# A new order for the preparation of the next head in the attention stage of a hybrid diffusion step

## The chip, the cores and the metric

One core of one Trainium2 chip runs the whole program. The metric is the device time of one execution in microseconds (us). TensorE is called PE below, VectorE DVE, ScalarE ACT, GpSimd POOL and SyncE SP; PEld is the weight load of PE.

## The reference

One transformer-like layer over 1024 latent and 128 context tokens, width 1024, in float32. It is: a modulated RMSNorm, one input projection, two branches (latent attention with 8 heads, and a gated linear recurrence), a gated merge, an output projection, and a convolutional gated MLP. Only the attention matters here:

```python
q  = (rmsnorm(pq, g_q) @ w_uq).reshape(B, T, 8, 64 + 32)       # rotary on the last 32, latent tokens only
kv = (ckv_keys @ w_ukv).reshape(B, K, 8, 64 + 64)               # keys (64) and values (64); K = 1152 for latents
s  = einsum('bqhd,bkhd->bhqk', q_nope, k_nope) + einsum('bqhr,bkr->bhqk', q_rope, k_rope)
p  = softmax(s * scale);  o = einsum('bhqk,bkhd->bqhd', p, v)
```

## The kernel before

The program runs its stages one after the other, with a barrier of all engines between them: setup, input projection with the recurrence, attention (`stage_attention`), merge, output projection with the MLP. The change touches the attention stage alone.

Float32 products are made as three products in a reduced format (high x high, high x low, low x high), so every operand is first split: ACT copies it to its high part, and DVE or POOL subtracts that to get the low part.

**A head's attention.** The keys are cut into tiles of 128. Unit `S k` (k = 0 to 8) computes the scores of key tile k with all 1024 latent queries, six matmuls of 512 columns into one half of a double buffer of PSUM (`ps_s`); ACT takes the exponential (L1707) and copies it to its high part (L1709). `L k` is the low part (L1743 on DVE for k = 0 to 3 and 9, L1756 on POOL for k = 4 to 8). `V k` multiplies the tile's values with it, six matmuls of 512 columns (L1688), added up in `ps_o`. `S 9`, `V 9` are the context queries, 128 columns wide. After `V 8` and after `V 9` ACT copies the result out of PSUM (`o_raw`, L1715 and L1718).

**The preparation of the next head.** While head h is computed, the units of head h + 1 are made, in `class HeadPrep`. All of them go through two PSUM banks that take turns (`ps_m`), in the order that is written in `PREP_UNITS`:

- `Q u` (u = 0 to 2, for 512, 512 and 128 queries): nine matmuls (L1407). ACT copies 64 rows (L1455), DVE does the rotation in three instructions (L1487, L1488, L1491). `H u` is its split on ACT (L1460) and POOL (L1522).
- `K u`: keys and values, six matmuls (L1414). ACT copies twice (L1465, L1467), POOL makes the low part.
- `M u` (16 of them) and `P u`: scores in one format pass only, for the maximum of each query; one matmul each for `M` (L1420), four small ones for `P` (L1427). DVE reduces each bank (L1500, L1502). `C` is that of the context queries (L1432, L1508).
- `X u`: transposes of the values (L1437), split by ACT (L1471) and DVE (L1496).
- `R u`: the maxima turned into a row (L1442, with twice as many records as matmuls written), taken by ACT (L1474) and then by DVE (L1514).

`W` is the split of the weights of the head after the next (L1568, L1569, L1571 on ACT, L1576 on POOL).

**What sets the order.** `HEAD_ITEMS` is one list for all engines: each engine walks through it and does its own part of each item, in that order. With two banks, the n-th preparation unit of `PREP_UNITS` can't start before the unit n - 2 has been taken out of its bank. The lines for this are

```python
n, _, _ = self.at[i, kind, u]
if n >= 2:
    self.taken(pe, *self.order[n - 2])
```

where `taken` waits for ACT (kinds Q, K, X, R) and for DVE (kinds Q, X, M, P, C, R). The first head has no head before it: `PREP_ALONE` prepares it alone, followed by `S 0` and `S 1` (written `("S", 10)` and `("S", 11)` where they belong to the next head). The last head has no preparation beside it.

Of the kernel before, what the change touches and what calls it, by code (L numbers as in the profile page):

```python
# [21 lines left out]
P = 128  # L22
# [609 lines left out]
def stage_project(nc, io, cst, base, upper, x_t, rb, h_hi, h_lo, after_x, low):  # L632


    with ExitStack() as ctx:
# [91 lines left out]
        with nc.Block() as block:  # L727
# [443 lines left out]
            def _(dve):  # L1171
# [163 lines left out]
                        item(kind, h, lv)  # L1335


PREP_UNITS = (("Q", 0), ("K", 0), ("Q", 1), ("K", 1), ("Q", 2), ("K", 2),
# [3 lines left out]
PREP_KINDS = "QKXMPCRH"  # L1342
PREP_ALONE = (("Q", 0), ("K", 0), ("H", 0), ("Q", 1), ("K", 1), ("H", 1), ("Q", 2), ("K", 2), ("H", 2)) + PREP_UNITS[6:]
HEAD_ITEMS = (
# [9 lines left out]
POOL_LO = (4, 5, 6, 7, 8)  # L1354
P_RING = 4

# [222 lines left out]
def stage_attention(nc, io, cst, lower, more, low):  # L1579
    with ExitStack() as ctx:  # L1580
# [9 lines left out]
        ps_oc = ps_s[1][:, 1, 0:TC]  # L1590
        order = [(h, kind, u) for h in range(HEADS) for kind, u in PREP_UNITS]
        prep = HeadPrep(sems, "prep", low, cst, b, ps_m, order)
# [12 lines left out]
        def heads(one):  # L1605

            for kind, u in PREP_ALONE + (("S", 10), ("S", 11)):
                one(kind, u, -1)
# [1054 lines left out]
```

## Time and profile before

| | us |
|---|---|
| median of three runs | 2312.3 (2308.95 to 2312.91) |
| the profiled execution | 2312.91 |
| its span, first to last instruction | 2311.1 |
| its mean granted PE clock | 0.961 of full speed |
| attention: first weight load of the preparation alone to the last `V` | 816.1 to about 1191 |
| busy share of the span: PE, DVE, ACT, POOL | 93%, 42%, 30%, 34% |

Times in the rows below are us from the first instruction. A row of the timeline has the start, the duration, the engine, the line, the operation and what it writes and reads, and a count where equal instructions that follow each other are merged; the brackets are the engine's idle time before it and what ended that. The ends of matmuls are modelled: a matmul of 512 columns shows about 0.40, but the next one starts 0.23 later, so the pace is to be read from starts.

### The profile page before, as it was taken

To read this page: it belongs to the slowest core of one execution; us is meant where nothing else is said; L and a number is where in the kernel's file an instruction comes from. 1 tells how busy PE (TensorE), PEld (TensorE's weight loads), DVE (VectorE), ACT (ScalarE), POOL (GpSimd) and SP (SyncE) were. 2 spreads that over 40 slices of the span, in tenths; PEclk is the share of its full clock that TensorE was granted. 3 is DMA by queue.
4 is the path that set the end of the run, shared out by engine and by line. 5 is a ranking of instruction groups with operands and counts; after the bars stand their busy time and mean duration, and the time that the engine had idled before them with its cause. 6 is when DMAs were issued, how large, how long until landed. Compare 5 with 4: busy or idle time off the path is not lost. (4 is left out here: it accounts for less than half of the span.)

```text
span 2311.1 us, 28777 instructions
## 1 busy us (share of the span) xinstructions
PE 2160.3 (93%) x11772; PEld 1967.3 (85%) x11772; DVE 973.3 (42%) x1422; ACT 703.4 (30%) x1028; POOL 795.0 (34%) x529
## 2 busy tenths in 40 slices
PE   7499999999999979999978878999999999999995
PEld 2479999999999947777758867899999999999994
DVE  3603444435133046556523416623343344423438
ACT  1234232323223146676655221212111211112120
POOL 0325262616123114544532642333322332223334
PEclk9699999999999969999989989999999999999998
DMA  6362111112211200000026372211111111111123
GB/s 230 109 210 86 31 51 44 47 41 61 75 38 53 77 15 16 16 31 16 11 103 184 107 150 82 83 55 46 46 37 37 55 37 46 31 52 46 41 69 128
DMA packets 147730, 155.72 MB, mean 67 GB/s; under 512 B 13703, under 2 KB 119760, under 8 KB 147600
## 3 DMA queue, kind: packets, MB, share of 16 engines
q1 hardware_dynamic: 146304, 149.17, 21.0%
q0 software_dynamic: 1296, 4.72, 0.5%
q8 instruction: 94, 1.54, 0.3%
q14 instruction: 36, 0.29, 0.0%
HBM read 127.23 MB, written 26.64 MB: 67 GB/s over the span
## 5 line engine op out<-in xcount | busy, mean ns | idle before, releaser
L129 POOL TENSOR_TENSOR s_w_lo<-s_w_raw,s_w_hi 128x1024 fp32r<-128x1024 f32 x86 | 220.0, 2559 | 528.0 <-ACT s_w_hi L124 528.0
L810 PE MATMUL s_psum<-h_hi,s_w_hi 128*128 128x384 f32 x1008 | 344.7, 345 | 26.9 <-POOL h_lo L250 26.9
L2321 PE MATMUL s_ps<-h_hi,s_w_hi 128*128 128x384 f32 x1056 | 353.4, 335 | 0.7 <-ACT gate_pad L2165 0.7
L2321 PE MATMUL s_ps<-h_hi,s_w_lo 128*128 128x384 f32 x1056 | 353.2, 334 | 0.0
L2321 PE MATMUL s_ps<-h_lo,s_w_hi 128*128 128x384 f32 x1056 | 353.2, 334 | 0.0
L810 PE MATMUL s_psum<-h_hi,s_w_lo 128*128 128x384 f32 x1008 | 338.2, 339 | 0.0
L810 PE MATMUL s_psum<-h_lo,s_w_hi 128*128 128x384 f32 x1008 | 338.1, 338 | 0.0
L810 PEld LDWEIGHTS s_psum<-h_hi,s_w_hi 128*128 128x128 f32 x1008 | 190.6, 190 | 36.9 <-issue 19.2
L2321 PEld LDWEIGHTS s_ps<-h_hi,s_w_hi 128*128 128x128 f32 x1056 | 198.4, 188 | 1.4 <-issue 1.0
L2321 PEld LDWEIGHTS s_ps<-h_lo,s_w_hi 128*128 128x128 f32 x1056 | 198.3, 188 | 0.3
L2321 PEld LDWEIGHTS s_ps<-h_hi,s_w_lo 128*128 128x128 f32 x1056 | 198.3, 188 | 0.0
L810 PEld LDWEIGHTS s_psum<-h_hi,s_w_lo 128*128 128x128 f32 x1008 | 192.1, 191 | 0.0
L810 PEld LDWEIGHTS s_psum<-h_lo,s_w_hi 128*128 128x128 f32 x1008 | 191.8, 190 | 0.0
L2496 DVE TENSOR_TENSOR yacc<-yacc,s_ps 128x512 f32<-128x512 f32 x144 | 99.0, 688 | 151.2 <-PE s_ps L2354 151.2
L2354 PE MATMUL s_ps<-w_lo,u_hi 128*128 128x512 f32 x360 | 140.4, 390 | 0.0
L2354 PE MATMUL s_ps<-w_hi,u_lo 128*128 128x512 f32 x360 | 140.3, 390 | 0.0
L2354 PE MATMUL s_ps<-w_hi,u_hi 128*128 128x512 f32 x360 | 140.1, 389 | 0.0
L2475 DVE SCALAR_TENSOR_TENSOR conv<-gate_pad,cols_b,conv 128x1154 f32<-128x1154 f32 x44 | 125.2, 2844 | 1.6
L2254 POOL TENSOR_TENSOR w_lo<-w_raw,w_hi 128x2048 fp32r<-128x2048 f32 x10 | 52.9, 5288 | 194.0 <-ACT w_hi L2188 194.0
L1756 POOL TENSOR_TENSOR p_lo<-prob,p_hi 128x1024 fp32r<-128x1024 f32 x40 | 95.6, 2389 | 60.8 <-ACT p_hi L1709 60.8
L1019 ACT ACTIVATE sig<-s_psum 128x384 f32<-128x384 f32 x72 | 35.1, 490 | 226.0 <-PE s_psum L810 226.0
L2248 POOL TENSOR_TENSOR u_lo<-conv,u_hi 128x1024 fp32r<-128x1024 f32 (+1 forms) x40 | 55.5, 1413 | 139.5 <-ACT u_hi L2176 139.5
(329 smaller groups left out, 4003.4 us busy)
## 6 DMA issues: line engine op xcount, KB each, us to landing
s_w_raw<-in_w_ffn_in SPq DMA_DIRECT2D x44, 512.0 KB, 3.7
s_w_raw<-in_w_in SPq DMA_DIRECT2D x41, 512.0 KB, 3.9
s_w_mod<-in_w_mod SPq DMA_DIRECT2D x8, 2048.0 KB, 8.2
w_raw<-in_w_ffn_out SPq DMA_DIRECT2D x11, 1024.0 KB, 4.8
scratch_gates<-sig SPq DMA_DIRECT2D x48, 192.0 KB, 1.9
merge_gates<-scratch_gates SPq DMA_DIRECT2D x16, 576.0 KB, 3.8
w_mod<-in_w_mod SPq DMA_DIRECT2D x4, 2048.0 KB, 10.5
scratch_o_mla<-o_raw SPq DMA_DIRECT2D x8, 576.0 KB, 3.1
```

The source lines that it names most:

```text
L129: pool.tensor_tensor(flat[0], flat[1], flat[2], ALU.subtract).then_inc(self.lo_ready, 1)
L810: return pe.matmul(bank(j), wx[c % 2][:, k, :], hx[:, k, j * CH:(j + 1) * CH], start=(k == 0 and n == 0), stop=(k == KD - 1 and n == 2))
L1019: act.activation(sigt[u % SIG_RING][:, :], bank(j), ACT.Sigmoid).then_inc(sig_done, 1)
L1756: pool.tensor_tensor(p_lo[u % P_RING][:, :], prob[u % 2][:, :], p_hi[u % P_RING][:, :], ALU.subtract).then_inc(lo_pool, 1)
L2248: last = pool.tensor_tensor(lo[:, src:src + n], conv[x][:, at:at + n], hi[:, src:src + n], ALU.subtract)
L2254: pool.tensor_tensor(w2_lo[:, :, :], w2_raw[:, :, :], w2_hi[:, :, :], ALU.subtract).then_inc(w2_lo_ready, 1)
L2321: mm = pe.matmul(ps[bank][:, 0:CH], a[s][:, k, :], b[:, k, j * CH:(j + 1) * CH], start=n == 0, stop=n == 3 * KD - 1)
L2354: mm = pe.matmul(bank[:, :], a[:, t * P:(t + 1) * P], b[:, half * HALF:(half + 1) * HALF], start=first and n == 0, stop=last and n == 3 * ...
L2475: dve.scalar_tensor_tensor(out, gpad[x][:, j:j + PAD - 2], cst.b("conv_w", 22 * j + n), out, ALU.mult, ALU.add).then_inc(conv_step, 1)
L2496: dve.tensor_tensor(dst, dst, ps[6 + n % 2][:, :], ALU.add).then_inc(y_added, 1)
```

## The change

Three lists are written in a new order; no instruction is added or taken out. In the preparation the three `Q` come before the three `K`, the 16 `M` come one to two tiles later in the head, and `X 1` and `X 2` come after `R 1` and `R 2`. The place of `S`, `L` and `V` relative to each other stays as it was, while `V 9`, `W` and `L 9` move relative to `R`.

```diff
-PREP_UNITS = (("Q", 0), ("K", 0), ("Q", 1), ("K", 1), ("Q", 2), ("K", 2),
+PREP_UNITS = (("Q", 0), ("Q", 1), ("Q", 2), ("K", 0), ("K", 1), ("K", 2),
               ("M", 0), ("M", 2), ("M", 4), ("M", 6), ("M", 1), ("M", 3), ("M", 5), ("M", 7), ("P", 0),
               ("M", 8), ("M", 10), ("M", 12), ("M", 14), ("R", 0), ("M", 9), ("M", 11), ("M", 13), ("M", 15), ("P", 1),
-              ("C", 0), ("X", 0), ("X", 1), ("R", 1), ("R", 2), ("X", 2))
+              ("C", 0), ("X", 0), ("R", 1), ("R", 2), ("X", 1), ("X", 2))
-PREP_ALONE = (("Q", 0), ("K", 0), ("H", 0), ("Q", 1), ("K", 1), ("H", 1), ("Q", 2), ("K", 2), ("H", 2)) + PREP_UNITS[6:]
+PREP_ALONE = (("Q", 0), ("Q", 1), ("H", 0), ("Q", 2), ("H", 1), ("K", 0), ("H", 2)) + PREP_UNITS[4:]
 HEAD_ITEMS = (
-    ("L", 0), ("S", 2), ("Q", 0), ("K", 0), ("L", 1), ("V", 0), ("H", 0), ("Q", 1), ("K", 1),
-    ("S", 3), ("L", 2), ("H", 1), ("Q", 2), ("K", 2), ("V", 1), ("M", 0), ("M", 2),
-    ("S", 4), ("L", 3), ("H", 2), ("M", 4), ("M", 6), ("V", 2), ("M", 1), ("M", 3),
-    ("S", 5), ("L", 4), ("M", 5), ("M", 7), ("V", 3), ("P", 0), ("M", 8),
-    ("S", 6), ("L", 5), ("M", 10), ("M", 12), ("V", 4), ("M", 14), ("R", 0),
-    ("S", 7), ("L", 6), ("M", 9), ("M", 11), ("V", 5), ("M", 13), ("M", 15),
-    ("S", 8), ("L", 7), ("P", 1), ("C", 0), ("V", 6), ("X", 0), ("X", 1),
-    ("S", 9), ("L", 8), ("V", 7), ("R", 1), ("R", 2), ("L", 9), ("W", 0), ("V", 8), ("X", 2), ("V", 9),
-    ("S", 10), ("S", 11))
+    ("L", 0), ("S", 2), ("Q", 0), ("L", 1), ("V", 0), ("Q", 1), ("H", 0),
+    ("S", 3), ("L", 2), ("Q", 2), ("V", 1), ("H", 1), ("K", 0),
+    ("S", 4), ("L", 3), ("H", 2), ("K", 1), ("V", 2), ("K", 2),
+    ("S", 5), ("L", 4), ("M", 0), ("M", 2), ("V", 3), ("M", 4), ("M", 6),
+    ("S", 6), ("L", 5), ("M", 1), ("M", 3), ("V", 4), ("M", 5), ("M", 7), ("P", 0),
+    ("S", 7), ("L", 6), ("M", 8), ("M", 10), ("V", 5), ("M", 12), ("M", 14), ("R", 0),
+    ("S", 8), ("L", 7), ("M", 9), ("M", 11), ("V", 6), ("M", 13), ("M", 15), ("P", 1),
+    ("S", 9), ("L", 8), ("C", 0), ("V", 7), ("X", 0), ("L", 9), ("W", 0), ("V", 8), ("R", 1), ("R", 2), ("V", 9), ("X", 1),
+    ("S", 10), ("X", 2), ("S", 11))
```

## Rows read from the trace of the kernel before

**Rows 1.** Stretches of the stage: us, each engine's busy time, granted PE clock, DMA.

```profile
946.00:1162.00 216.00, 215.56 (x1062) 171.71 (x1063) 125.44 (x205) 144.20 (x213) 103.32 (x60) 1.00 0.06 20
1162.00:1192.00 30.00, 26.71 (x117) 21.02 (x116) 7.25 (x6) 21.23 (x25) 11.99 (x5) 1.00 0.05 20
833.00:845.00 12.00, 9.31 (x21) 4.25 (x21) 10.17 (x15) 0.31 (x2) 2.29 (x3) 0.62 0.01 1
```

**Rows 2.** Timeline of PE: first matmul of `S 0` of heads 0, 1 and 7.

```profile
857.20 0.78 PE L1672 MATMUL ps_s<-q_hi,k_hi 97*128 97x512 f32 x1
...
903.17 0.45 PE L1672 MATMUL ps_s<-q_hi,k_hi 97*128 97x512 f32 x1
...
1162.15 0.45 PE L1672 MATMUL ps_s<-q_hi,k_hi 97*128 97x512 f32 x1
```

**Rows 3.** Waits of PEld, 857 to 1160: total us, times, longest.

```profile
PEld ps_m L1420 <- DVE att_tops L1500: 4.0, 14, 0.4
...
PEld ps_m L1420 <- ACT qf L1455: 1.5, 7, 0.2
PEld ps_s L1685 <- DVE p_lo L1743: 1.2, 6, 0.2
```

**Rows 4.** Timeline of PE: `M 1` and `M 3`, `S 5`, `M 5` and `M 7`, `V 3`.

```profile
923.85 0.99 PE L1420 MATMUL ps_m<-k_hi,q_hi 96*128 96x512 f32 x2
924.68 0.39 PE L1672 MATMUL ps_s<-q_hi,k_hi 97*128 97x512 f32 x1
...
926.05 0.63 PE L1420 MATMUL ps_m<-k_hi,q_hi 96*128 96x512 f32 x2
926.52 0.63 PE L1688 MATMUL ps_o<-p_hi,v_hi 128*128 128x512 f32 x2
```

**Rows 5.** Timeline of DVE: reductions of `M 4, 6, 1, 3`, then of `M 5, 7`.

```profile
923.00 2.58 DVE L1500 TENSOR_REDUCE att_tops<-ps_m 128x1 f32<-128x512 f32 x4
926.48 1.29 DVE L1500 TENSOR_REDUCE att_tops<-ps_m 128x1 f32<-128x512 f32 x2 [0.90 <-PE ps_m L1420]
```

**Rows 6.** Timeline of PEld: loads of `M 1`, `M 3` and `S 5`.

```profile
923.74 0.19 PEld L1420 LDWEIGHTS ps_m<-k_hi,q_hi 96*128 96x128 f32 x1 [0.16 <-DVE att_tops L1500]
924.34 0.19 PEld L1420 LDWEIGHTS ps_m<-k_hi,q_hi 96*128 96x128 f32 x1 [0.41 <-DVE att_tops L1500]
924.45 0.19 PEld L1672 LDWEIGHTS ps_s<-q_hi,k_hi 97*128 97x128 f32 x1
```

**Rows 7.** Timeline of PE at a head's end: `R 1` and `R 2`, `V 8`, `X 2`, `V 9`.

```profile
942.92 1.25 PE L1442 MATMUL ps_m<-ident,att_maxima 128*1 128x128 f32 x10
944.10 0.74 PE L1688 MATMUL ps_o<-p_hi,v_hi 128*128 128x512 f32 x2
...
945.62 0.38 PE L1437 MATMUL ps_m<-ident,kvf 128*128 128x128 f32 x2
945.93 0.33 PE L1685 MATMUL ps_s<-p_hi,v_hi 128*128 128x128 f32 x1
```

**Rows 8.** Timelines of ACT, DVE and POOL at the same head's end.

```profile
943.99 0.74 ACT L1474 ACTIVATE q_hi<-ps_m 1x512 fp32r<-1x512 f32 x2 [1.78 <-PE ps_m L1442]
944.76 0.24 ACT L1568 ACTIVATE hw_raw<-hw_raw 128x48 f32<-128x48 f32 x1
...
945.16 0.74 ACT L1571 ACTIVATE hw_hi<-hw_raw 128x640 fp32r<-128x640 f32 x1
945.82 1.03 ACT L1715 ACTIVATE o_raw<-ps_o 128x1024 f32<-128x1024 f32 x1
...
944.68 0.88 DVE L1514 SCALAR_TENSOR_TENSOR q_lo<-ps_m,q_hi 1x512 fp32r<-1x512 f32 x2 [2.46 <-ACT q_hi L1474]
...
940.67 2.40 POOL L1756 TENSOR_TENSOR p_lo<-prob,p_hi 128x1024 fp32r<-128x1024 f32 x1 [1.31 <-ACT p_hi L1709]
```

**Rows 9.** Timelines of DVE and PE at a head's start: `L 0`, `V 0`.

```profile
906.97 1.23 DVE L1743 TENSOR_TENSOR p_lo<-prob,p_hi 128x1024 fp32r<-128x1024 f32 x1 [2.39 <-ACT p_hi L1709]
...
910.80 0.62 PE L1688 MATMUL ps_o<-p_hi,v_hi 128*128 128x512 f32 x2
```

**Rows 10.** The preparation alone: first `M` reductions, then `R` on ACT, `X 2` on PE.

```profile
834.33 2.63 DVE L1500 TENSOR_REDUCE att_tops<-ps_m 128x1 f32<-128x512 f32 x4
...
855.42 0.74 ACT L1474 ACTIVATE q_hi<-ps_m 1x512 fp32r<-1x512 f32 x2 [1.68 <-PE ps_m L1442]
...
856.89 0.66 PE L1437 MATMUL ps_m<-ident,kvf 128*128 128x128 f32 x2 [1.08 <-ACT q_hi L1474]
```

## The prediction

> **What bounds the kernel now.** First the stretches of the attention stage [rows 1]: from 946 to 1162 us PE is busy for 215.56 of 216 us at full clock, DVE for 125, ACT for 144, POOL for 103. So here every us in which PE stands still lengthens the program, and work taken off another engine gains nothing unless PE waited for it. Second, the pace of a head, from the first matmul of `S 0` to that of the next head [rows 2]: 1162.15 - 903.17 is six heads, 43.16 us each. Head 0 took 903.17 - 857.20 = 45.97. Seven heads have a preparation beside them, and only they and the preparation alone are changed. Third, what PE waited for inside those heads [rows 3]: the loads of `M` for DVE's reductions 4.0 us in 14 waits, for ACT's copy of `Q 2` 1.5 us, and the loads of `V 9` for `L 9` 1.2 us. That is 6.7 us in all seven heads, and it is nearly all that a better order could give back, since the matmuls stay the same in number and shape.
>
> **The order, part by part.** What decides is the rule of the two banks: unit n waits until unit n - 2 has been taken. So I write down the units that PE meets with nothing between them. Before, no run between two `S` or `V` has more than two units whose results go to a slow reader: `M 1, M 3`, then `S 5`, `M 5, M 7`, then `V 3`, and so on. The new list has three such units in a row in three places: `M 5, M 7, P 0` before `S 7`; `M 12, M 14, R 0` before `S 8`; `M 13, M 15, P 1` before `S 9`. The third waits for the reduction of the first.
>
> *Price of a run of three.* `M 5` starts at 926.05 [rows 4] and its reduction at 926.48 [rows 5], 0.43 later. Two reductions take 1.29, so one is 0.645. The four from 923.00 in 2.58 end one at 923.65 and one at 924.29, and the loads that waited start at 923.74 and 924.34 [rows 6], 0.05 to 0.10 later; the matmul comes 0.11 after its load (923.74 and 923.85 [rows 4, 6]). So the third unit starts 0.43 + 0.645 + 0.07 + 0.11 = 1.26 after the first. Two `M` need 926.52 - 926.05 = 0.47 [rows 4]. PE stands still for 1.26 - 0.47 = 0.79. Three times a head: 2.37. Bounds: 0.6 if the load is hidden, 0.9 if the reduction is late. The reductions have nothing queued ahead of them on DVE there (`L 5` to `L 7` are POOL's), so the first of each run starts at once.
>
> Are the waiting units passed by others in PE's queue? `S 5`'s load stands at 924.45, after the load of `M 3` that had waited until 924.34 [rows 6]; at that time `S 5` itself had nothing to wait for. The queue kept its order across a wait. The Trainium skill, TensorE: Matmul & The Clock Gate, section "Architectural detail: the array is 16× 32×32, not 1× 128×128", says that PE's queue is a partial reorder window that pulls weight loads ahead of matmuls in flight. Taken as far as past a waiting unit, that rule of the Trainium skill would hide these stalls behind the next `S`, 2.37 less a head; the row, 924.45 after 924.34, does not show it.
>
> *The head's end.* The new order is `V 7, X 0, W, V 8, R 1, R 2, V 9, X 1, S 0`. `X 1` now waits until `R 1` is taken by ACT and then DVE. On ACT, `R 1` now stands behind the eviction of `V 8`. Count from the start of `V 8`. Its eviction started 945.82 - 944.10 = 1.72 later [rows 7, 8]. `W`, 944.76 to 945.90 on ACT, moves ahead of `V 8` and ends at about the same 1.7 after `X 0`'s copy, so I keep 1.72. The eviction lasts 1.03 and the next copy begins as it ends: `R 1` on ACT at 2.72. DVE followed it by 944.68 - 943.99 = 0.69 and needs most of 0.88 for the two, say 0.68 for the long one. The load follows 0.05 later and the matmul 0.11 after that: 2.72 + 0.69 + 0.68 + 0.16 = 4.25. PE itself is through with `V 8` (945.62 - 944.10 = 1.52), `R 1, R 2` (944.10 - 942.92 = 1.18) and `V 9` (0.40, up to the next `S 0` at 903.17 + 43.16) at 3.10. Stall: 1.15. Bounds: 0.6 (ACT lets `R 1` in early) and 1.5 (`W` late, eviction later by 0.3). `X 2` behind `S 0` then finds its bank free, so nothing more is lost there.
>
> *What is given back.* `M 1, M 3` took 924.68 - 923.85 = 0.83 instead of 0.47 because `L 3` stood between the reductions: with `M` moved behind `S 5`, 0.36 a head. The wait on `Q 2`'s copy goes, about 0.1, since `K 1` and `K 2` lie a whole tile back. `L 9` on DVE now comes before `R`, so `V 9` doesn't wait: 0.12. In all 0.6 a head. It can't be more than 6.7 / 7 = 0.96 [rows 3], nor much less than 0.3.
>
> *What costs nothing.* `K` units moved behind `V 1` and `V 2` are read by ACT and POOL only, and first needed by `M` a whole tile later. `V 0` is now only `Q 0` behind `S 2`, about 1.4 earlier; `L 0` was done at 908.20 and `V 0` started at 910.80 [rows 9], so 2.6 of cover become 1.2. `V 8` needs `L 8`, done at 943.07 for a start at 944.10 [rows 7, 8]; between `S 8` and `V 8` PE has about 0.5 less work of its own but 0.79 more of standing still, so the cover stays. If either cover were gone, it would cost its shortfall, at most some tenths a head. The DMAs of `W` are issued by SP with no new wait before them.
>
> *The preparation alone.* There the `M` are paced by DVE anyway. The second `Q` no longer waits, but `K 0` waits for it on DVE; I expect the first reductions, now 834.33 [rows 10], 0.3 earlier. At the end `R 1` starts about 1.2 earlier, as `X 1` no longer stands before it, but `X 1` and `X 2` then follow: `X 2` was at 856.89, 1.47 after ACT's start on `R` at 855.42 [rows 10], and now another unit of about 0.9 stands after that same wait. Net 0.3. Together -0.6, between +1 and -2.
>
> **The sum.** 2.37 + 1.15 - 0.6 = 2.92 a head, 46.1 in place of 43.16. Seven heads: +20.4. With -0.6: +19.8. The profiled execution took 2312.91, its span 2311.1 and 1.8 around it, 0.6 above the median of 2312.3. 2312.9 + 19.8 = 2332.7; against the median, 2332.1. I say 2332.5.
>
> **The rivals.**
>
> 1. *Faster: only the waits on DVE and ACT go, PE's queue passes the waiting unit.* The place is the third unit of a run; the gain is the 0.6 a head and 0.6 alone: 2312.9 - 4.2 - 0.6 = 2308.1. It decides if the three runs and `X 1` together cost less than 0.6 a head. Against it speaks the order of loads [rows 6]. Chance 4%. The rule of the Trainium skill, TensorE: Matmul & The Clock Gate, on loads pulled ahead, read that far, is this rival and its 2308.1.
> 2. *No change within 0.2%* (4.6 us, which is about what a measurement of this kernel can tell from none): the waits cost about 0.6 to 1.2 a head, and what is given back covers them. It would need reductions that start well before a matmul's end, against 0.43 at 926.48 [rows 5]. About 2314. Chance 6%.
> 3. *Half of it.* Either the runs of three or the head's end costs, not both: without the end (2.37 - 0.6) x 7 - 0.6 = +11.8, 2324.7; without the runs (1.15 - 0.6) x 7 - 0.6 = +3.3, which falls under rival 2. Chance of the first 10%.
> 4. *The clock falls.* In 833 to 845 us, with PE busy 9.31 of 12 in single `M`s with gaps, the mean granted clock was 0.62, between the two levels of 1.2 and 2.4 GHz; in 1162 to 1192, busy 26.71 of 30 with waits of up to an us, it stayed at full speed [rows 1]. The new heads stand still for 3.5 of 46 us, a smaller share than in the second row, but the stalls gather between `S 6` and `S 9`. If each head fell to half for as long as at head 0's start, it would cost 45.97 - 43.16 = 2.8 each [rows 2]: 2332.5 + 19.6 = 2352. Chance 4%.
> 5. *A cover that is gone* (`V 0`, `V 8` or `R 1` on ACT late by 0.5 to 0.8 more): +3.5 to +5.6, 2336 to 2338. It lies in the forecast's own range.
>
> **How the numbers follow.** The forecast with rival 5 holds 76%: 2332.5, with its own bounds per head of 1.8 + 0.6 - 0.9 = 1.5 and 2.7 + 1.5 - 0.3 = 3.9, that is +10.5 - 2 and +27.3 + 1: 2321 to 2341. Rival 3's first case lies in it. The range is 2320 to 2342, which leaves out rivals 1, 2 and 4, 14%, and a little of the tails. Faster 4%, same 6%, slower 90%.
>
> **What would show it.** In the timeline of a head: `S 0` to `S 0` about 46.1. `P 0`, `R 0` and `P 1` with a wait of their load of 0.7 to 0.8, put down to L1500, 21 times in all; `X 1` with one of about 1.1, put down to L1474 or L1514, seven times; the waits of [rows 3] on `M` and of `V 9` gone. PE's busy time as before, its clock at full speed from 870 to 1190. DVE's, ACT's and POOL's busy time unchanged. The stages after the attention shifted as a whole. The forecast is wrong if PE's load for `S 7` stands before that of `P 0`, if the reduction starts much sooner than 0.43 after the matmul, or if a clock below 1.00 shows in the middle of the stage.

## The result and the profile after

The changed kernel is slower: 2327.4 us median (2326.67 to 2330.14, four runs) against 2312.6 (2308.95 to 2314.75, four runs), a ratio of 1.0067 with a 95% interval of 1.005 to 1.0086. The forecast was 2332.5, range 2320 to 2342. The profiled execution took 2326.68 with a span of 2324.9, 13.8 more than before.

Stretches, with the columns of [rows 1]. The first fence is the program's first 200 us of the kernel before; the second is the changed kernel's first 200 us and the same stretch of the stage as in [rows 1]:

```profile
0.00:200.00 200.00, 150.29 (x776) 108.31 (x777) 67.68 (x79) 61.92 (x86) 47.09 (x34) 0.88 0.51 176
```

```profile
0.00:200.00 200.00, 150.25 (x785) 108.34 (x786) 69.09 (x79) 63.33 (x89) 48.55 (x35) 0.90 0.51 176
946.00:1162.00 216.00, 204.82 (x998) 163.83 (x999) 123.71 (x193) 139.51 (x203) 93.64 (x57) 1.00 0.06 20
```

PE, busy for 215.56 of 216 us before, is now busy for 204.82, at full clock (by the modelled ends of its matmuls; by their starts it loses more, as the sums below show). Where, the waits of its loads from 853 to 1176 us show (total us, times, longest), which answer to [rows 3]:

```profile
PEld ps_m L1427 <- DVE att_tops L1500: 13.8, 14, 1.0
PEld ps_m L1437 <- ACT q_hi L1474: 7.0, 7, 1.0
PEld ps_m L1442 <- DVE att_tops L1500: 6.9, 7, 1.0
```

`P 0` and `P 1` wait 14 times and `R 0` 7 times for the reduction of the first unit of their run, `X 1` 7 times for `R 1`. The prediction had 21 waits put down to L1500 and 7 to L1474 or L1514, and so they stand here, though it had those of `P` and `R 0` at 0.7 to 0.8 and not at 1.0. The waits of `M` and `V 9` of [rows 3] are gone. A load's wait, up to 1.0 here, is longer than the 0.71 that PE loses, because loads run ahead of matmuls. What PE loses is seen in starts. First PE, then DVE, at `M 5, M 7, P 0, S 7`, answering to [rows 4, 5]:

```profile
927.88 0.63 PE L1420 MATMUL ps_m<-k_hi,q_hi 96*128 96x512 f32 x2
929.06 0.66 PE L1427 MATMUL ps_m<-k_hi,q_hi 96*128 96x128 f32 x4 [0.55 <-DVE att_tops L1500]
929.56 0.45 PE L1672 MATMUL ps_s<-q_hi,k_hi 97*128 97x512 f32 x1
...
928.31 1.29 DVE L1500 TENSOR_REDUCE att_tops<-ps_m 128x1 f32<-128x512 f32 x2 [0.57 <-PE ps_m L1420]
```

`P 0` starts 1.18 after `M 5` in place of 0.47: a loss of 0.71. The bracket's 0.55 is idle time by modelled ends. The reduction starts 0.43 after `M 5`, as in [rows 5].

The head's end, answering to [rows 7, 8]: `V 8`; `R 1, R 2`; `V 9`; `X 1`; `S 0`; then ACT's eviction of `V 8` and its `R`, and DVE's `R`:

```profile
942.27 0.71 PE L1688 MATMUL ps_o<-p_hi,v_hi 128*128 128x512 f32 x2
...
943.84 1.25 PE L1442 MATMUL ps_m<-ident,att_maxima 128*1 128x128 f32 x10
945.02 0.33 PE L1685 MATMUL ps_s<-p_hi,v_hi 128*128 128x128 f32 x1
...
945.29 0.27 PE L1685 MATMUL ps_s<-p_hi,v_lo 128*128 128x128 f32 x1
946.46 0.63 PE L1437 MATMUL ps_m<-ident,kvf 128*128 128x128 f32 x4 [0.90 <-ACT q_hi L1474]
946.85 0.48 PE L1672 MATMUL ps_s<-q_hi,k_hi 97*128 97x512 f32 x1
...
943.94 1.02 ACT L1715 ACTIVATE o_raw<-ps_o 128x1024 f32<-128x1024 f32 x1
944.99 0.74 ACT L1474 ACTIVATE q_hi<-ps_m 1x512 fp32r<-1x512 f32 x2
...
945.68 0.88 DVE L1514 SCALAR_TENSOR_TENSOR q_lo<-ps_m,q_hi 1x512 fp32r<-1x512 f32 x2 [2.02 <-ACT q_hi L1474]
```

The last matmul of `V 9` starts at 945.29 and takes PE 0.11, so 1.06 is lost before `X 1`.

The first matmuls of `S 0` of heads 0, 1 and 7, answering to [rows 2]:

```profile
853.67 0.78 PE L1672 MATMUL ps_s<-q_hi,k_hi 97*128 97x512 f32 x1
...
901.05 0.48 PE L1672 MATMUL ps_s<-q_hi,k_hi 97*128 97x512 f32 x1
...
1175.89 0.48 PE L1672 MATMUL ps_s<-q_hi,k_hi 97*128 97x512 f32 x1
```

From the starts of the two traces the whole difference can be laid out. First matmul of the stage: 816.10 before, 813.06 after; last of `V 9`: 1190.5 and 1204.6.

| part | before | after | difference |
|---|---|---|---|
| up to the attention | 816.1 | 813.1 | -3.0 |
| preparation alone | 41.10 | 40.61 | -0.5 |
| head 0 | 45.97 | 47.38 | +1.4 |
| heads 1 to 6 | 6 x 43.16 | 6 x 45.81 | +15.9 |
| head 7, to the last `V 9` | 28.3 | 28.7 | +0.4 |
| all that follows | 1120.7 | 1120.3 | -0.4 |
| span | 2311.1 | 2324.9 | +13.8 |

The attention alone is 17.2 longer. The 3.0 before it are no work of the change: the instructions there are the same, the clock of the first 200 us was 0.88 in one execution and 0.90 in the other, and over the nine other traces of this study the stage's first matmul lies between 812.6 and 817.0, whatever the kernel. So experiments are read below by the pace of a head as well, from one `S 9` to the next over heads 0 to 6, which repeats within 0.05 us from head to head (0.07 in the kernel with the new end, and in that with two units each the first head is 0.35 longer than the others); the program's time spreads by 12 to 14 us over the runs of the kernel before that stand beside the experiments.

### The profile page after: what moved, and what is told of

Same layout as the page of the kernel before. It is cut to its first block and busy times, and to the rows that moved or that the text cites. A ratio compares the mean times of both kernels' runs of the same rounds, so it can differ in the third digit from the quotient of the medians.

```text
span 2324.9 us, 28777 instructions
## 1 busy us (share of the span) xinstructions
PE 2155.3 (93%) x11772; PEld 1962.1 (84%) x11772; DVE 978.6 (42%) x1422; ACT 705.3 (30%) x1028; POOL 789.6 (34%) x529
## 5 line engine op out<-in xcount | busy, mean ns | idle before, releaser
L1500 DVE TENSOR_REDUCE att_tops<-ps_m 128x1 f32<-128x512 f32 x128 | 83.0, 687 | 65.9 <-PE ps_m L1420 65.6
```

The lines of the kernel that those rows point to most:

```text
L1500: dve.tensor_reduce(b.tops[:, t, j:j + 1], ps[:, :], axis=AX.X, op=ALU.max).then_inc(self.m_dve, 1)
```

## The experiments

| kernel | us a head | program, us | ratio to before, 95% |
|---|---|---|---|
| before | 43.16 | 2312.6 | |
| changed | 45.81 | 2327.4 | 1.005 to 1.0086 |
| changed, `R` before `V 8` | 45.01 | 2322.7 | 1.003 to 1.0056 |
| changed, `V 8` evicted after `R` | 45.70 | 2326.8 | 1.0043 to 1.0076 |
| changed, `X 1` behind `S 0` | 45.18 | 2322.1 | 1.0039 to 1.0088 |
| changed, two units each | 45.31 | 2329.3 | 1.0066 to 1.0096 |
| before, one run of three | 44.03 | 2318.8 | 1.0009 to 1.0037 |
| before, three runs of three | 45.61 | 2325.1 | 1.0042 to 1.0088 |
| before, new end of a head | 44.82 | 2320.5 | 1.0037 to 1.0065 |
| before, small waits removed | 42.53, again 42.50 | 2307.4, again 2307.9 | 0.9974 to 1.0002, again 0.9967 to 0.9998 |

Each ratio is to runs of the kernel before on the same chip, whose medians were not all the same: 2308.3 beside the kernels with two units each, with the new end, and the first of the last row; 2313.2 beside `X 1` behind `S 0` and the second of the last row; 2312.9 beside the other four experiments.

**One run of three in the kernel before.**

```diff
-    ("S", 5), ("L", 4), ("M", 5), ("M", 7), ("V", 3), ("P", 0), ("M", 8),
+    ("S", 5), ("L", 4), ("M", 5), ("M", 7), ("P", 0), ("V", 3), ("M", 8),
```

> The kernel before with P 0 ahead of V 3, which makes one run of three units. Theory (two banks): P 0's load waits, PE loses 0.71 us a head, 43.16 becomes 43.87, the program gains 5.0: 2317.5. Rival (what costs in the changed kernel is the crowding of M and DVE's load in the later tiles, not the run): no change, 2312.5.

44.03 a head, 0.87 more, and a ratio of 1.0023. PE in its timeline at `M 5, M 7, P 0, V 3`:

```profile
927.48 0.63 PE L1420 MATMUL ps_m<-k_hi,q_hi 96*128 96x512 f32 x2
928.66 0.66 PE L1427 MATMUL ps_m<-k_hi,q_hi 96*128 96x128 f32 x4 [0.55 <-DVE att_tops L1500]
929.16 0.68 PE L1688 MATMUL ps_o<-p_hi,v_hi 128*128 128x512 f32 x2
```

Again 1.18 from the first unit to the third, 0.71 lost. Of the other 0.16, 0.10 is `P 0` itself, which takes 929.16 - 928.66 = 0.50 and not 0.40 (927.91 to 928.31 in the kernel before): after a wait the loads of its four short matmuls haven't run ahead. The last 0.06 isn't laid out. Swapping two neighbours in the list was enough; `M` stayed where they were, so crowding isn't needed.

**Three runs of three in the kernel before.** `P 0` ahead of `V 3`, `M 14` ahead of `V 4`, `P 1` ahead of `S 8`:

```diff
-    ("S", 5), ("L", 4), ("M", 5), ("M", 7), ("V", 3), ("P", 0), ("M", 8),
-    ("S", 6), ("L", 5), ("M", 10), ("M", 12), ("V", 4), ("M", 14), ("R", 0),
-    ("S", 7), ("L", 6), ("M", 9), ("M", 11), ("V", 5), ("M", 13), ("M", 15),
-    ("S", 8), ("L", 7), ("P", 1), ("C", 0), ("V", 6), ("X", 0), ("X", 1),
+    ("S", 5), ("L", 4), ("M", 5), ("M", 7), ("P", 0), ("V", 3), ("M", 8),
+    ("S", 6), ("L", 5), ("M", 10), ("M", 12), ("M", 14), ("V", 4), ("R", 0),
+    ("S", 7), ("L", 6), ("M", 9), ("M", 11), ("V", 5), ("M", 13), ("M", 15), ("P", 1),
+    ("S", 8), ("L", 7), ("C", 0), ("V", 6), ("X", 0), ("X", 1),
```

> The kernel before with three runs of three units: P 0 ahead of V 3, M 14 ahead of V 4, P 1 ahead of S 8. Theory (two banks): three waits of 0.71 a head, less about 0.05: 45.25 a head, +14.7, 2327. If waits after each other absorb one another, less than 10. Rival as for one run: 2312.5.

45.61, that is 2.45 more, or 0.82 a run against 0.87 for one: the stalls add up and don't absorb each other.

**The new end of a head in the kernel before.**

```diff
-    ("V", 6), ("X", 0), ("X", 1),
-    ("S", 9), ("L", 8), ("V", 7), ("R", 1), ("R", 2), ("L", 9), ("W", 0), ("V", 8), ("X", 2), ("V", 9),
-    ("S", 10), ("S", 11))
+    ("V", 6), ("X", 0),
+    ("S", 9), ("L", 8), ("V", 7), ("L", 9), ("W", 0), ("V", 8), ("R", 1), ("R", 2), ("V", 9), ("X", 1),
+    ("S", 10), ("X", 2), ("S", 11))
```

(and `R 1, R 2` before `X 1` in `PREP_UNITS`, as in the changed kernel.)

> The kernel before with the changed kernel's end of a head alone (V 8, R 1, R 2, V 9, X 1, then S 0, X 2, S 1, and L 9 earlier). Theory: X 1 waits 1.06 us a head, V 9's small wait goes: 43.16 + 1.0 = 44.1, +6.6, 2319. Rival (the wait needs the delays of the three runs before it): under 0.4 a head, 2314.

44.82, 1.66 more where 1.0 was expected. The wait of `X 1` is there without any run of three. A second one came with it, in the waits of the loads from 853 to 1176 and on PE between the last of `V 7` and `V 8`:

```profile
PEld ps_m L1437 <- ACT q_hi L1474: 8.6, 8, 1.6
PEld ps_o L1688 <- POOL p_lo L1756: 6.9, 7, 1.0
```

```profile
941.86 0.62 PE L1688 MATMUL ps_o<-p_hi,v_lo 128*128 128x512 f32 x2
943.05 0.73 PE L1688 MATMUL ps_o<-p_hi,v_hi 128*128 128x512 f32 x2 [0.57 <-POOL p_lo L1756]
...
946.09 0.27 PE L1685 MATMUL ps_s<-p_hi,v_lo 128*128 128x128 f32 x1
947.26 0.63 PE L1437 MATMUL ps_m<-ident,kvf 128*128 128x128 f32 x4 [0.90 <-ACT q_hi L1474]
```

`V 7`'s last two matmuls, begun at 941.86, take 0.46, so PE stands still for 0.73 before `V 8`, and for 947.26 - 946.20 = 1.06 before `X 1`. With 0.12 given back by `V 9` this makes 1.67 of the measured 1.66. The 1.06 is exactly that of the changed kernel, so the new end brings it with it. The 0.73 is rival 5's lost cover: without `R 1, R 2` ahead of it, `V 8` comes before POOL is through with `L 8`. The changed kernel has `R` behind `V 8` too, and waits for nothing there. `L 8` on POOL, in the changed kernel and then in this one:

```profile
938.89 2.36 POOL L1756 TENSOR_TENSOR p_lo<-prob,p_hi 128x1024 fp32r<-128x1024 f32 x1 [3.15 <-ACT p_hi L1709]
```

```profile
940.60 2.40 POOL L1756 TENSOR_TENSOR p_lo<-prob,p_hi 128x1024 fp32r<-128x1024 f32 x1 [1.32 <-ACT p_hi L1709]
```

In both, `L 8` is done 6.2 to 6.3 after PE begins `S 8` (941.25 - 934.99 and 943.00 - 936.81). From there to `V 8` PE takes 942.27 - 934.99 = 7.28 in the changed kernel, and here 942.32 - 936.81 = 5.51 before it stands still. The difference is four `M` (4 x 0.23), which stand a tile earlier here, and `P 1`'s stall with its 0.10 (0.81). So the cover of 1.02 in the changed kernel is made of work and of a stall, and by this count (an estimate, no run tries it) 0.2 of it would be left without the stall. So the end alone costs 1.66 here, and in the changed kernel 1.06 less what is given back: the 0.73 depends on what stands before the end.

**`R` before `V 8` in the changed kernel.** Theory: `X 1` waits because `R 1` is issued too late for its two readers. Rival: it would wait there anyway.

```diff
-    ("V", 7), ("X", 0), ("L", 9), ("W", 0), ("V", 8), ("R", 1), ("R", 2), ("V", 9), ("X", 1),
+    ("V", 7), ("X", 0), ("R", 1), ("R", 2), ("L", 9), ("W", 0), ("V", 8), ("X", 1), ("V", 9),
```

> The changed kernel with R 1 and R 2 put back before V 8 and X 1 after V 8; all else stays. Theory (the two banks): X 1's wait of 1.06 us a head goes, as V 8 stands between R 1 and X 1, and a wait of about 0.2 comes at R 2 for X 0: a head takes about 44.9 us instead of 45.80, the program 2321. Rival (the later place of M and the new order of Q and K cost the time, the end is a by-product): the head stays at 45.8 and the program at 2327.

45.01 a head, 0.80 less than the changed kernel. In the waits of the loads from 853 to 1176 the seven of the heads are gone; the one of the preparation alone is left:

```profile
PEld ps_m L1437 <- ACT q_hi L1474: 1.6, 1, 1.6
```

`V 8`'s 1.5 us of matmuls now cover the readers. That it isn't 1.06 is seen on PE at `R 1, R 2, V 8`:

```profile
944.35 1.50 PE L1442 MATMUL ps_m<-ident,att_maxima 128*1 128x128 f32 x10
945.78 0.73 PE L1688 MATMUL ps_o<-p_hi,v_hi 128*128 128x512 f32 x2
```

`R 1, R 2` take 1.43 there and 1.18 at the end (945.02 - 943.84), because `X 0` stands right before them and `R 2` is then the third of a run. 1.06 - 0.25 = 0.81.

**`V 8` evicted after `R`, on ACT only.** The prediction had put the length of `X 1`'s wait down to ACT, on which the eviction of `V 8` stands before `R 1`. Here PE's list stays and ACT takes the eviction after `R 2`:

```diff
+    if kind == "V" and u == 8 and h < HEADS - 1: return
...
+    if kind == "R" and u == 2 and h >= 0: kind, u = "V", 8
```

> The changed kernel with ACT's eviction of V 8 moved behind its copies of R 1 and R 2, on ACT alone. If the eviction is what delays R 1 (as the prediction put it), X 1's wait falls from 1.06 us to 0.2 to 0.5, 44.9 to 45.2 a head, 2321 to 2323. If it is R 1's own way (matmuls, ACT, DVE) that is too long for the 0.4 us of V 9 between it and X 1, the wait falls by 0.1 at most, and the program stays at 2327.

45.70, 0.11 less. The wait of `X 1`'s load stays: 6.5 us in 7 from 857 to 1180, 0.9 each where it was 1.0. ACT, then PE around it:

```profile
945.11 0.74 ACT L1571 ACTIVATE hw_hi<-hw_raw 128x640 fp32r<-128x640 f32 x1
946.80 0.74 ACT L1474 ACTIVATE q_hi<-ps_m 1x512 fp32r<-1x512 f32 x2 [0.95 <-PE ps_m L1442]
...
945.73 1.25 PE L1442 MATMUL ps_m<-ident,att_maxima 128*1 128x128 f32 x10
...
948.27 0.63 PE L1437 MATMUL ps_m<-ident,kvf 128*128 128x128 f32 x4 [0.81 <-ACT q_hi L1474]
```

ACT now stood idle for 0.95 and still took `R 1` only at 946.80, 1.07 after PE began it; `X 1` came 1.47 later. `R 1`'s own way, 1.07 + 1.47 = 2.54, is longer than what PE has to do meanwhile, `R 1, R 2, V 9`, 1.18 + 0.38. The eviction adds only 944.99 - 943.84 - 1.07 = 0.08. The prediction named the wrong cause for a wait whose size it had nearly right. [rows 7, 8] had `R 1`'s own way already: 943.99 - 942.92 = 1.07 from PE to ACT, and 1.47 from ACT to the next `X` in [rows 10].

**`X 1` behind `S 0`.**

```diff
-    ("R", 1), ("R", 2), ("V", 9), ("X", 1),
-    ("S", 10), ("X", 2), ("S", 11))
+    ("R", 1), ("R", 2), ("V", 9),
+    ("S", 10), ("X", 1), ("X", 2), ("S", 11))
```

> The changed kernel with X 1 moved behind S 0, where X 2 already stands; nothing else. Theory (R 1's own way is longer than what PE has between R 1 and X 1): S 0's 1.4 us now cover it, the wait of 1.06 goes, 45.80 becomes 44.7 to 44.8 a head, the program 2319 to 2321. X 1 and X 2 are both taken before ACT's exponential of S 1, so L 0 is not late. Rival (as in the kernel with two units each, where V 0 then waited 0.86 for L 0): 45.6 a head, no gain.

45.18, 0.63 less where 1.0 was expected. `X 1` no longer waits; the second half of `S 0` does. PE, then DVE:

```profile
945.68 0.40 PE L1672 MATMUL ps_s<-q_hi,k_lo 97*128 97x512 f32 x1
946.26 0.47 PE L1672 MATMUL ps_s<-q_hi,k_hi 97*128 97x512 f32 x1 [0.19 <-DVE q_lo L1514]
...
945.43 0.88 DVE L1514 SCALAR_TENSOR_TENSOR q_lo<-ps_m,q_hi 1x512 fp32r<-1x512 f32 x2 [2.03 <-ACT q_hi L1474]
```

946.26 - 945.68 - 0.23 = 0.35 lost. `R` writes the row of `q_hi` and `q_lo` that `S 0` multiplies, so this much is left when `R` stands behind `V 8` and `S 0` follows `V 9`. It makes the gain 1.06 - 0.35 = 0.71; the other 0.08 isn't laid out. In the changed kernel `X 1`'s longer wait lies over it. The prediction had no such term, and for the changed kernel needed none.

**Two units each in the middle.** The same units as in the changed kernel, spread so that no three stand together, on its new start of a head:

```diff
-    ("S", 6), ("L", 5), ("M", 1), ("M", 3), ("V", 4), ("M", 5), ("M", 7), ("P", 0),
-    ("S", 7), ("L", 6), ("M", 8), ("M", 10), ("V", 5), ("M", 12), ("M", 14), ("R", 0),
-    ("S", 8), ("L", 7), ("M", 9), ("M", 11), ("V", 6), ("M", 13), ("M", 15), ("P", 1),
-    ("S", 9), ("L", 8), ("C", 0), ("V", 7), ("X", 0), ("L", 9), ("W", 0), ("V", 8), ("R", 1), ("R", 2), ("V", 9), ("X", 1),
-    ("S", 10), ("X", 2), ("S", 11))
+    ("S", 6), ("L", 5), ("M", 1), ("M", 3), ("V", 4), ("M", 5), ("M", 7),
+    ("S", 7), ("L", 6), ("P", 0), ("M", 8), ("V", 5), ("M", 10), ("M", 12),
+    ("S", 8), ("L", 7), ("M", 14), ("R", 0), ("V", 6), ("M", 9), ("M", 11),
+    ("S", 9), ("L", 8), ("M", 13), ("M", 15), ("V", 7), ("P", 1), ("C", 0), ("L", 9), ("W", 0), ("V", 8), ("X", 0), ("R", 1), ("V", 9), ("R", 2),
+    ("S", 10), ("X", 1), ("S", 11), ("X", 2))
```

> The changed kernel with its new start of a head (all Q before K, M behind S 5), but never three slow units in a row later, and R 1 ahead of V 9 with X 1 behind S 0. Theory (the new start costs nothing, only the runs and the end do): the waits of 3 x 0.71 + 1.06 go, a wait of about 0.35 comes at M 13: 43.0 to 43.3 a head, 2308 to 2313. Rival (the start costs too): 44 or more a head, 2318 or more.

A miss: 45.31 where 43.0 to 43.3 was expected. The waits of runs of three are gone and three others stand in the same table, from 853 to 1176:

```profile
PEld ps_m L1420 <- ACT q_hi L1474: 7.2, 7, 1.0
PEld ps_o L1688 <- DVE p_lo L1743: 7.0, 6, 1.5
...
PEld ps_m L1420 <- DVE att_tops L1500: 2.9, 7, 0.4
```

The first is `M 11`, two units behind `R 0`; ACT and PE there:

```profile
934.09 1.06 ACT L1709 ACTIVATE p_hi<-prob 128x1024 fp32r<-128x1024 f32 x1
935.17 0.59 ACT L1474 ACTIVATE q_hi<-ps_m 1x512 fp32r<-1x512 f32 x1
...
935.63 0.40 PE L1420 MATMUL ps_m<-k_hi,q_hi 96*128 96x512 f32 x1
936.65 0.47 PE L1420 MATMUL ps_m<-k_hi,q_hi 96*128 96x512 f32 x1 [0.62 <-issue]
```

`R 0` is taken by ACT behind the two long instructions of `S 8`: 936.65 - 935.63 - 0.23 = 0.79 lost. The second is `V 0`, which waits for `L 0` on DVE, behind `X 2` taken late by ACT: 0.86. `M 15` loses 0.37 for `M 11`'s reduction (the third line), and `R 2`, the third of `X 0, R 1, R 2`, 0.24: 2.26 in all. The small waits of the kernel before don't stand in this one, so the kernel to compare with is the last one below, 42.53 a head: 45.31 is 2.78 more, and some 0.5 of it isn't laid out. So "no three in a row" isn't sufficient: two are enough if a reader has other work queued ahead. That the crowding of the changed kernel costs what it does is shown by the waits and by the runs of one and three, not by this kernel. The new start of a head costs nothing by the changed kernel's own trace, where no wait stands between `S 0` and `M 5`.

**The kernel before with its small waits removed.** If 0.6 a head can be given back, it must be there without the new order. `L 3` goes ahead of `M 0, M 2`, `H 1` behind `V 1`, `L 9` ahead of `R` (the expectation's `H 1` behind `K 2` is its place behind `V 1`, which follows `K 2`):

```diff
-    ("S", 3), ("L", 2), ("H", 1), ("Q", 2), ("K", 2), ("V", 1), ("M", 0), ("M", 2),
-    ("S", 4), ("L", 3), ("H", 2),
+    ("S", 3), ("L", 2), ("Q", 2), ("K", 2), ("V", 1), ("H", 1), ("L", 3), ("M", 0), ("M", 2),
+    ("S", 4), ("H", 2),
...
-    ("V", 7), ("R", 1), ("R", 2), ("L", 9),
+    ("V", 7), ("L", 9), ("R", 1), ("R", 2),
```

> The kernel before with L 3 ahead of M 0 and M 2, H 1 behind K 2 and L 9 ahead of R 1: only the small waits of the kernel before are taken away, no unit of PE is moved. By its waits 0.36 + 0.1 + 0.12 us a head: 42.6 a head, 4.1 less, 2308.5. If L 3 earlier only moves the wait, 43.1 and no change.

42.53 a head, 0.63 less. Its stretch of 920 to 1130:

```profile
920.00:1130.00 210.00, 210.00 (x1050) 169.87 (x1049) 127.15 (x203) 143.49 (x213) 103.50 (x59) 1.00 0.06 20
```

PE is busy for all of it, and the waits of [rows 3] on `M` and `V 9` are gone. How much each of the three moves gives back wasn't tried apart. The same kernel once more:

> The same kernel as b4_tuned, timed again because its first interval (0.9974 to 1.0002) left open whether it is faster at all. Its head of 42.53 us against 43.16 says 4.4 less in seven heads: a ratio of 0.998. If the unchanged stages or the preparation alone take it back, 1.000.

42.50 a head and a ratio of 0.9983 [0.9967, 0.9998], after 0.9988 [0.9974, 1.0002]. 7 x 0.65 = 4.5 us of 2310 is 0.9980, and both intervals hold it. It is the fastest kernel of the study, and by the pace of a head, 42.5 against 43.16 in both traces, the gain is beyond its repetition of 0.05; the program's time alone shows it barely.

## Why the prediction was right, step by step

The forecast of 2332.5 is 5.1 above the median, and the measured 2327.4 lies in the range. For the attention, +19.8 was forecast and +17.2 came.

- **Runs of three.** Forecast 0.79 each. Measured 0.71, and 0.10 for the four short matmuls behind the wait: 0.81 a run, or 0.82 to 0.87 by the kernels with one run and three. The term 0.11 from load to matmul was too much: the third unit's matmul starts with its load, both at 929.06. The bare 0.71 and the added 0.10 make up the same sum by chance.
- **The head's end.** Forecast 1.15, measured 1.06. The size was right and the reason wrong: not ACT's eviction of `V 8` (0.08) but `R 1`'s own way through PE, ACT and DVE (2.54), as the kernel with the eviction moved shows.
- **Given back.** Forecast 0.6; measured 45.81 - 43.16 = 2.65 = 3 x 0.71 + 1.06 - 0.54, or 0.74 if the 0.10 of `P 0` and of `P 1` is counted as a loss. By itself, in the kernel with the small waits removed, it is 0.63 to 0.66.
- **Head.** +2.92 forecast, +2.65 measured. The stage was forecast 2.6 too long: 6 x 0.27 = 1.6 of it are heads 1 to 6, and 1.5 head 0, less some 0.5 for head 7 and the preparation.
- **Clock.** Rival 4 fell: the granted clock was 1.00 from 870 to 1190 us, with stalls of 0.71 three times and one of 1.06 within 18 us of each head. Head 0 grew by 1.4 only, not by 2.65; the half-speed stretch reached 5.7 us into it before and 3.6 us after, see below. 2.1 us less at half speed are about 1.05 us, most of the missing 1.24. The prediction had no such term.
- **Covers.** `V 0`: `L 0` is done at 906.87 and `V 0` starts at 907.54, 0.67 of cover where 1.2 was forecast. `V 0` came 1.14 earlier after `S 0` (6.49 in place of 7.63), and `L 0` 0.79 later (5.82 in place of 5.03), which the prediction hadn't counted: on DVE it now stands behind `X 2`, from 905.44 to 905.73. `V 8` kept its cover, as forecast and for the reason given, 1.02 after 1.03: less work of PE's before it, and `P 1`'s stall in its place.
- **Rivals 1, 2, 3.** No load passed a waiting one. The load of `P 0` that waited stands at 929.06 and the first of `S 7`, which had nothing to wait for, behind `P 0`'s other loads:

```profile
929.06 0.52 PEld L1427 LDWEIGHTS ps_m<-k_hi,q_hi 96*128 96x128 f32 x4 [0.98 <-DVE att_tops L1500]
929.50 0.19 PEld L1672 LDWEIGHTS ps_s<-q_hi,k_hi 97*128 97x128 f32 x1
```

  By the Trainium skill, TensorE: Matmul & The Clock Gate, section "Architectural detail: the array is 16× 32×32, not 1× 128×128", PE's queue is a partial reorder window, which can pull weight loads ahead of matmuls in flight. This trace agrees: `M 7`'s load begins at 927.89, while `M 5`'s matmul, begun at 927.88, holds PE until 928.12. It shows no load past one that waits, and in each of the eleven traces the first 1500 loads after 816.5 us stand in the order of their matmuls. Both parts cost, which the kernels with the one and the other show separately.
- **Preparation alone.** -0.6 forecast, -0.5 in the profiled pair, which doesn't confirm it. The same old preparation took 39.6 to 42.3 over the five traces that have it, the new one 39.1 to 40.8 over its five; the means are 41.2 and 40.4, nearer together than the traces of one kind. The granted clock in it differs, too: 0.62 from 816 to 857 us in the kernel before, 0.74 in the one with three runs of three.

What the prediction left out and what didn't matter: head 7 grew by 0.4, and the stages before the attention differed by 3.0 in the profiled pair without any work of the change. The profiled difference of 13.8 is that much, and 0.4 behind the stage, smaller than the stage's 17.2; the medians' difference of 14.8 is measured over other executions, and how much of the same spread is in it stays open.

## What to carry to other kernels

Where results leave through two buffers in turn, write down the units that the writer meets with nothing long between them: a third in a row costs the first one's reader's delay and time less the second unit's own work, here 0.43 + 0.65 + 0.1 - 0.47, and swapping two neighbours in a list is enough to make it. Count also two in a row whose reader has long work queued ahead, and ask of every cover whether it is made of work or of another stall, since removing one stall can then bring up the next, as `S 0`'s 0.35 came up when `X 1`'s wait was taken away. Where the program's time spreads by more than the change, judge by the pace of a repeated part in the trace.

## What the runs showed of the hardware beyond this

The half-speed stretch after the preparation isn't the same length in each trace. `S 0` of head 0, before, after and with three runs of three (in the first two fences the last matmul that takes 0.4 to the next start, and the first after which it is 0.23; in the third the first two of all):

```profile
862.90 0.57 PE L1672 MATMUL ps_s<-q_lo,k_hi 97*128 97x512 f32 x1
863.31 0.40 PE L1672 MATMUL ps_s<-q_hi,k_lo 97*128 97x512 f32 x1
```

```profile
857.24 0.55 PE L1672 MATMUL ps_s<-q_hi,k_lo 97*128 97x512 f32 x1
857.62 0.39 PE L1672 MATMUL ps_s<-q_hi,k_hi 97*128 97x512 f32 x1
```

```profile
852.69 0.47 PE L1672 MATMUL ps_s<-q_hi,k_hi 97*128 97x512 f32 x1
853.00 0.40 PE L1672 MATMUL ps_s<-q_lo,k_hi 97*128 97x512 f32 x1
```

Of the two levels, 1.2 and 2.4 GHz, the higher came, read from these starts, 5.7 us after `S 0` began in the first, 3.6 us in the second, and before `S 0` in the third; in the other traces 2.7 to 3.6 us after. At the lower level a start comes only every 0.43 us, so these figures can be 0.4 too small; the granted clock shows 0.50 from 857.20 to 863.20 and 1.00 from 863.30 in the first. Five of the traces, of the kernel before, those with one run and three runs of three, and the two with the small waits removed, have the same program up to there, and still it came 5.7, 3.1, 3.1 and 2.7 us after `S 0` and once before it. So the 2.1 us between the two kernels need no work of the change. What sets it wasn't tried.
